# Second block's gate and up products with the weights stationary: 18 of 22 chunks in another form, no turns of their activations

## The reference, cut

```python
def swiglu(x, wg, wu, wd):
    return (jax.nn.silu(x @ wg) * (x @ wu)) @ wd
...
x = x + 0.5 * rms_norm(swiglu(rms_norm(x, g_ffn1_pre[l]), ffn1_wg[l], ffn1_wu[l], ffn1_wd[l]),
                       g_ffn1_post[l])
```

## Time and profile before

| | us |
|---|---|
| median of 3 runs | 2007.19 (2004.69 to 2007.57) |
| the profiled execution, its own time | 2004.62 |
| its span, first to last instruction | 2002.8 |
| PE busy | 1989.1 (99%) |
| DVE busy | 1209.0 (60%) |
| ACT busy | 991.7 (50%) |
| POOL busy | 300.8 (15%) |

### The profile page before, as it was taken

One profiled execution on the slowest core, in us unless ns is written; L12 is line 12 of the kernel. 1 busy time (PEld: TensorE's weight loads), 2 busy tenths in 40 slices (PEclk: granted clock), 3 DMA queues, 4 the chain that ended last, 5 costly groups with the idle time before them and its releaser, 6 DMA issues.

```text
span 2002.8 us, 26838 instructions
## 1 busy us (share of the span) xinstructions
PE 1989.1 (99%) x11298; PEld 1722.4 (86%) x11298; DVE 1209.0 (60%) x1163; ACT 991.7 (50%) x1076; POOL 300.8 (15%) x204
## 2 busy tenths in 40 slices
PE   9999999999999999999999999999999999999998
PEld 8899999999988888888888888888888888888887
DVE  6854446756677565546566875546555555686453
ACT  6754334345444454445366564445444535666443
POOL 4134401514244010002100110001000210011000
PEclk9999999999999999999999999999999999999999
DMA  7345546534555555555543545555555554364553
GB/s 224 106 130 183 171 172 209 170 127 148 174 185 188 191 187 188 189 192 167 188 128 125 199 158 185 185 198 168 189 180 198 168 168 147 120 208 152 183 179 136
DMA packets 195585, 343.64 MB, mean 172 GB/s; under 512 B 14122, under 2 KB 97356, under 8 KB 195356
## 3 DMA queue, kind: packets, MB, share of 16 engines
q1 hardware_dynamic: 194844, 340.12, 51.6%
q0 software_dynamic: 368, 0.79, 0.2%
q10 hardware_dynamic: 272, 1.26, 0.2%
HBM read 341.10 MB, written 1.05 MB: 171 GB/s over the span
## 4 chain that ended last, share of the span: by engine, by line
PE 88%; DVE 5%; ACT 3%; DMA 2%; issue 1%; POOL 1%; SPq 0%; DVEq 0%; POOLq 0%
PE banks L591 18%; PE banks L594 17%; PE banks L592 17%; PE banks L409 5%; PE banks L469 5%; PE banks L403 3%; PE banks L402 3%; PE banks L401 3%; PE banks L410 3%; PE banks L1833 2%; PE banks L1834 2%; PE banks L1835 2%; DVE w_lo L395 1%; ACT w_hi L379 1%; PE banks L630 1%; DVE xn_both L852 1%
## 5 line engine op out<-in xcount | busy, mean ns | idle before, releaser
L395 DVE TENSOR_TENSOR w_lo<-raw,w_hi 128x2048 fp32r<-128x2048 f32 x307 | 730.0, 2381 | 512.3 <-ACT w_hi L379 512.0
L379 ACT ACTIVATE w_hi<-raw 128x2048 fp32r<-128x2048 f32 x311 | 594.1, 1914 | 642.5 <-DMA raw<-ffn_wd 149.8
L591 PE MATMUL banks<-w_hi,xn_both 128*128 128x512 f32 x1192 | 472.0, 396 | 1.3 <-DVE xn_both L852 0.7
L592 PE MATMUL banks<-w_lo,xn_both 128*128 128x512 f32 x1192 | 464.1, 389 | 0.0
L594 PE MATMUL banks<-w_hi,xn_both 128*128 128x512 f32 x1192 | 459.6, 390 | 0.0
L591 PEld LDWEIGHTS banks<-w_hi,xn_both 128*128 128x128 f32 x1192 | 223.9, 188 | 50.4 <-DVE w_lo L395 3.1
L594 PEld LDWEIGHTS banks<-w_hi,xn_both 128*128 128x128 f32 x1192 | 223.8, 188 | 47.6
L592 PEld LDWEIGHTS banks<-w_lo,xn_both 128*128 128x128 f32 x1192 | 224.1, 188 | 44.0
L591 PE MATMUL banks<-w_hi,act_both 128*128 128x512 f32 x352 | 138.1, 392 | 0.0
L592 PE MATMUL banks<-w_lo,act_both 128*128 128x512 f32 x352 | 137.0, 389 | 0.0
L409 PE MATMUL banks<-xn_both,w_hi 128*128 128x512 f32 x352 | 123.5, 394 | 0.5 <-DVE ffn_u L1002 0.5
(11 more groups left out here) (384 smaller groups left out, 3348.7 us busy)
## 6 DMA issues: line engine op xcount, KB each, us to landing
raw<-w_in SPq DMA_DIRECT2D x58, 1024.0 KB, 5.1
raw<-ffn_wd SPq DMA_DIRECT2D x44, 1024.0 KB, 4.8
raw<-ffn_w_gu SPq DMA_DIRECT2D x42, 1024.0 KB, 5.0
raw<-ffn_wu SPq DMA_DIRECT2D x40, 1024.0 KB, 5.0
raw<-ffn_wg SPq DMA_DIRECT2D x35, 1024.0 KB, 5.0
raw<-ret_w_in SPq DMA_DIRECT2D x24, 1024.0 KB, 5.0
raw<-ffn_w_down SPq DMA_DIRECT2D x22, 1024.0 KB, 4.8
raw<-ret_w_out SPq DMA_DIRECT2D x8, 1024.0 KB, 5.3
```

The source lines that it names most:

```text
L379: nc.scalar.activation(hi_of(n0), raw_of(n0), ACT.Copy).then_inc(hi_done(n0), 1)
L395: nc.vector.tensor_tensor(lo_of(n0), raw_of(n0), hi_of(n0).bitcast(F32), ALU.subtract).then_inc(lo_done(n0), 1)
L591: pe.matmul(ps[:, (b + n) * 512:(b + n + 1) * 512], xh, h, start=start, stop=False)
L592: pe.matmul(ps[:, (b + n) * 512:(b + n + 1) * 512], xh, o, start=False, stop=False)
```

## The change

In each of the four feed-forwards chunks 4 to 21 (`NTILE` = 18) take the first block's form: a chunk is 1024 rows by 256 columns, even ones gate, odd ones up, and `tile_pair` issues 16 `joined` pairs into one pair of banks. Chunks 0 to 3 (the first 512 hidden columns) stay as they were, with the only `turn` that is left, after chunk 8. DVE, ACT and POOL get the first block's tile steps (`tile_gate`, `tile_up`, `tile_silu`, `tile_hi`, `pool_xffn`). They are placed in step c, behind the split of chunk c + 2, on tile c - 4, which is chunk c. The norm's factor is now needed along the free axis too, so there is a third matmul after chunk 3 with 256 columns, a square root and a reciprocal of 256 columns.

```diff
+            def tile_pair(n):
+                n0, b = base + 4 + n, ring(f, 2 + n)
+                wait_split(n0)
+                if n == 1:
+                    pe.wait_ge(S["gsil"], 2 * fi + 2)
+                elif n == 2:
+                    pe.wait_ge(S["gact"], 2 * fi + 2)
+                elif n:
+                    pe.wait_ge(S["sums"], x_sums(fi, n - 3))
+                for m in range(2):
+                    for kt in range(KT):
+                        last = joined(pe, b + m, slot_of(n0), kt * 256 + m * P, xn_both, slice(kt * T2, (kt + 1) * T2),
+                                      kt == 0, kt == KT - 1)
+                last.then_inc(S["pe_chunk"], 1)
...
-            for u in range(1, 11):
-                for q in range(2):
...
-                    if u >= 4 and u % 2 == 0 and q == 0:
-                        turn(u // 2 - 2)
...
+            pe.matmul(ps[:, 7 * 512 + T2:8 * 512], ones, sacc[:, 0:T2], start=False, stop=True, skip_group_check=True).then_inc(S["stat"], 1)
+            for n in range(NTILE):
+                tile_pair(n)
+                if n == 4:
+                    turn()
...
+                if k < 2:
+                    pe.wait_ge(S["fl"], 2 * fi + 2)
+                else:
+                    pe.wait_ge(S["al"], pair_count(fi, k - 2))
...
-                if k < 2:
-                    turn(4 + k)
...
+            def tile_silu(p):
+                act.wait_ge(S["g1"], pair_count(fi, p))
+                act.activation(xg[:, p % 2, :], xg[:, p % 2, :], ACT.Silu).then_inc(S["silu"], 1)
+
+            def tile_hi(p):
+                act.wait_ge(S["act"], pair_count(fi, p))
+                o = (4 + 2 * p) * T2
+                act.activation(act_hi[:, o:o + 2 * T2], xg[:, p % 2, :], ACT.Copy).then_inc(S["ah"], 1)
...
-                elif c in (6, 10, 14, 18, 22):
-                    silu((c - 2) // 4)
-                if c in (9, 13, 17, 21, 23, 24):
-                    hidden_hi((9, 13, 17, 21, 23, 24).index(c))
+                    silu()
+                if 4 <= c < 4 + NTILE:
+                    (tile_hi if c % 2 else tile_silu)((c - 4) // 2)
+                if c == 9:
+                    hidden_hi()
...
+            def leave(n, out):
+                dve.wait_ge(S["pe_chunk"], base + 4 + n + 1)
+                dve.tensor_reduce(out, bank(ring(f, 2 + n), 2).rearrange("p b (h t) -> p b t h", t=T2), AX.X, ALU.add).then_inc(S["sums"], 1)
+                dve.wait_ge(S["sums"], x_sums(fi, n))
+
+            def tile_gate(p):
+                if p >= 2:
+                    dve.wait_ge(S["al"], pair_count(fi, p - 2))
+                g = tiles(xg[:, p % 2, :], T2)
+                leave(2 * p, g)
+                dve.tensor_tensor(g, g, rep(rstd[:, 0:T2], 2, T2), ALU.mult).then_inc(S["g1"], 1)
+
+            def tile_up(p):
+                leave(2 * p + 1, tiles(xu[:, :], T2))
+                dve.wait_ge(S["silur"], pair_count(fi, p))
+                dve.tensor_tensor(xg[:, p % 2, :], xg[:, p % 2, :], xu[:, :], ALU.mult).then_inc(S["act"], 1)
...
+                    dve.reciprocal(rstd[:, 0:T2], std[:, 0:T2]).then_inc(S["sums"], 1)
                     dve.wait_ge(S["rstd"], s + 1)
...
+                    gated()
+                    dve.wait_ge(S["sums"], x_sums(fi, -1))
+                if 4 <= c < 4 + NTILE:
+                    (tile_up if c % 2 else tile_gate)((c - 4) // 2)
+                if c == 9:
+                    hidden_lo()
+
+        def pool_xffn(f):
+            for p in range(TPAIR):
+                g, v, o = xg[:, p % 2, :], pair_count(f - 2, p), (4 + 2 * p) * T2
+                pool.wait_ge(S["silu"], v)
+                pool.tensor_tensor(tiles(g, T2), tiles(g, T2), rep(rstd[:, 0:T2], 2, T2), ALU.mult).then_inc(S["silur"], 1)
+                pool.wait_ge(S["ah"], v)
+                pool.tensor_tensor(act_lo[:, o:o + 2 * T2], g, act_hi[:, o:o + 2 * T2].bitcast(F32), ALU.subtract).then_inc(S["al"], 1)
...
+            for n in range(NTILE):
+                at = 512 + 256 * (n // 2)
+                load(sp, base + 4 + n, 0, (uv if n % 2 else gv)[:, :, at:at + 256], (KT, 256))
```

More of the change, by code:

```diff
@@ L48 @@
 HEAD_SUMS = 4
+X_SUMS = HEAD_SUMS + 2 * NPAIR + KT
 AHEAD = 2
@@ new lines, in pe_xffn @@
+            for q in range(2):
+                for tb in range(2):
+                    if f > 2 and (q, tb) == (0, 0):
+                        continue
+                    last = quarter(base + 2 + q, 1, q, tb, False)
+                    if tb:
+                        last.then_inc(S["pe_chunk"], 1)
+                    elif q:
+                        last.then_inc(S["gmm"], 1)
+            if f == 2:
+                pe.wait_ge(S["hacc"], 8 * 4)
+            else:
+                pe.wait_ge(S["sa2"], 3 * (j + 1))
@@ L665, in pe_xffn @@
+            for tb in range(2):
+                pe.matmul(ps[:, 7 * 512 + 2 * tb:7 * 512 + 2 * tb + 2], sacc[:, tb * P:tb * P + P], ones[:, 0:2],
+                          start=(tb == 0), stop=True, skip_group_check=True)
+            pe.matmul(ps[:, 7 * 512 + T2:8 * 512], ones, sacc[:, 0:T2], start=False, stop=True, skip_group_check=True).then_inc(S["stat"], 1)
[3 more added lines that the diff above has]
+                    turn()
             a0, _, a1, _ = down_banks(f)
@@ L772, in gated, with hidden_lo @@
+                    dve.wait_ge(S["gsil"], 2 * fi + tb + 1)
+                    b = (ring(f, 1) + tb) * 512
+                    x = gs[:, tb, :]
+                    dve.scalar_tensor_tensor(out=x, in0=ps[:, b:b + 512], scalar=rcol[:, tb:tb + 1], in1=x, op0=ALU.mult,
                                              op1=ALU.mult).then_inc(S["gact"], 1)
-            def hidden_lo(g):
-                n = 4 if g < NGRP - 1 else 2
+            def hidden_lo():
                 for tb in range(2):
-                    dve.wait_ge(S["fh"], 12 * fi + 2 * g + tb + 1)
+                    dve.wait_ge(S["fh"], 2 * fi + tb + 1)
@@ L937, in sp_xffn @@
             base = BASE[f"gu{f}"]
-            for c in range(20):
+            for c in range(4):
                 if base + c in EXTRA:
                     continue
[L941 to L949, removed]
+                q, v = c % 2, uv if c >= 2 else gv
+                load(sp, base + c, 0, v[:, 4 * q:4 * q + 4, 0:512], (4, 512))
+            for n in range(NTILE):
+                at = 512 + 256 * (n // 2)
+                load(sp, base + 4 + n, 0, (uv if n % 2 else gv)[:, :, at:at + 256], (KT, 256))
             sp_wide(BASE[f"dn{f}"], w_dn.rearrange("(k p) c -> p k c", p=P), NDN, 0, 0)
```

79 lines of the change are left out of this document (35 added, 44 removed).

## The result

The changed kernel takes **2063.28 us** (median of 4 runs, 2060.0 to 2063.62), the kernel before 2007.38 beside it (median of 4, 2004.69 to 2007.98). The ratio is 1.0277, with a 95% interval of 1.0264 to 1.029: slower by 2.8%, where 2069 was forecast and 2055 to 2088 was the range. The profiled execution of the changed kernel took 2063.3 us, its span is 2061.5 us and its clock 0.996.

A forecast was written before the change was run, and what follows sets the result against it. TensorE's matmul count by spacing was taken to bound the kernel. A closed VectorE-ScalarE ring would add 15.5 us in each of four feed-forwards, +62 us: 2066.6 against the profiled execution, plus 2.6 for the median, forecast 2069 us, range 2055 to 2088.

The forecast's parts named there:

- What bounds the kernel before: Whole kernel: TensorE's matmul count by their spacing; chunks of 5.44 us in the old form, 5.55 in the new.
- PE's own count: TensorE per feed-forward: slower gate/up chunks, fewer transposes, one new norm product; -1.75 us each, -7 us in all.
- the product with the ones matrix: New 256-column norm matmul after chunk 3 in each feed-forward: 0.35 us taken as added.
- The ring: Gate/up chunks: VectorE drain, ScalarE tile step and high part, VectorE split, next drain wait in a circle; chance 0.86.
- The period: Time from drain to drain in the ring: 6.69 us gate, 6.83 up, mean 6.76, against TensorE's chunk of 5.55.
- Where it starts: gu3: VectorE free for the first drain at 1197.9 us, after the split, reciprocals and gated products.
- PE's waits: TensorE idles for w_lo about 1.2 us per chunk, from chunk 11 or 12 to 24 of each feed-forward.
- The clock: Rival: pauses drop TensorE to 1.2 GHz for a third of the ringed chunks; +87 us more, 2156 us; chance 0.02.
- The total: Four feed-forwards, gu2 to gu5, at +15.5 us each: +62 us, giving a forecast of 2069 us.
- the prediction's own bound of 7.1 us: Longest drain-to-drain time, with no overlap of neighbours and the full 1.36 and 0.83 us; 24 us more in all.

The follow-up runs named there:

- e2: Changed kernel with VectorE's tile step ahead of the split of chunk c + 2 from step 5, and hidden_lo behind that split; 1998.35 us, ratio 0.9965 to before.
- e1: Changed kernel with VectorE's tile step ahead of the split of chunk c + 2 from step 5, hidden_lo left in place; 2007.88 us, ratio 1.0008 to before.
- e3: Changed kernel with only ScalarE reordered: high part of chunk c + 3 ahead of the tile step of chunk c; 1998.39 us, ratio 0.9963 to before.
- e4: Changed kernel with one more ScalarE copy of 128 x 512 in every tile step, read by nobody; 2098.75 us.
- e5: e2 with the extra ScalarE copies of e4; 1999.13 us, ratio 0.9968 to the kernel before.
- e6: Changed kernel with both VectorE's order of e2 and ScalarE's order of e3; 2000.3 us, ratio 0.9968 to the kernel before.

## Why the prediction was right, point by point

- **What bounds the kernel before** held: chunk times by the starts (5.44, 5.55) came out again: 5.55 in the changed kernel (1221.11 - 1215.56, chunk 5) and in e2.
- **One reading was too strong**: that PE never waits for these steps in the first block. The earlier trace rows have one wait of 0.5 us, which the prediction names further on, and nothing hung on it.
- **PE's own count.** -1.75 us per feed-forward; e2, where nothing else is late, shows -1.77 in gu3. Inside, one term was a little too small: the product with the ones matrix was taken at 0.35 plus 0.1, and chunk 4 is 6.43 us from end to end (1215.56 - 1209.13) instead of 5.90 before, which is +0.53 with the 0.107 of the new form in it. So the product itself cost 0.42.
- **The ring** closed where it was said, through the steps that were said, and e1 to e3 show that the order closes it and e4 that its length is the chunk time.
- **The period** was the mis-sized term: 6.76 us forecast, 6.66 measured. The gate half was worked out at 6.69 and came at 6.64. The up half was at 6.89, of which 0.2 was the first block's longer way from reduction to product and silu; 0.14 of it was kept (6.83), so 0.07 in the mean of 6.76. In the unrolled code it is all gone (1.26 and 0.72 again). The other 0.03 is spread over the rows' distances, which came 0.01 to 0.03 shorter. 18 x 0.1 = 1.8 us per feed-forward too much.
- **Where it starts** came out by some luck. The first drain was set 6.7 us behind the end of chunk 3 (1197.9 - 1191.2), and came 7.1 behind (1216.22 against 1209.13). Under that lie two errors of opposite sign. The split of chunk 6, ahead of the first drain, was taken as in the kernel before, done 3.2 us behind the end of chunk 3, and was done 4.1 behind (1213.27), since ACT had waited for its load until 1209.11. The reciprocals and gated products behind it were given 3.5 us and took 2.95 (1216.22 - 1213.27); 0.15 of that is a slip, as the prediction's own terms from 1194.43 give 1197.75 and not 1197.9. From the first drain to the start of chunk 24: 120.9 us (forecast 122.8, with 1.1 for `hidden_hi`, measured 0.97 as the gap 1249.51 to 1257.14 less 6.66). From there to the end of chunk 28: 27.6 (forecast 27.5). Forecast 15.5, then +0.4, -1.9, +0.1 is 14.1.
- **PE's waits** began at chunk 12, as worked out.
- **The clock** did fall once, for about 3.4 us behind the 1.81 us wait in gu3, and it cost nothing, since the ring hid it: chunk 13 began without a wait, chunk 14 behind 0.22 instead of 0.84 us, and the drains stayed 6.66 apart. That is the self-limiting price which the rival named; its +87 us needed a fall in every third chunk, and took 11.1 us for a slow chunk, where 16 pairs at the measured 0.64 us make 10.2. The Trainium skill, page "TensorE: Matmul & The Clock Gate", section "A second HAM failure mode: psum-queue depth-cycling", tells of a bf16 kernel in which short pauses between groups of matmuls swing the clock. Here the regular pauses of 0.74 to 0.91 us never did: the granted clock is 1.00 over 1262 to 1337 us and over the same stretch of the other three feed-forwards.
- **The total**: 4 x 15.5 = 62 against 55.1 in these stretches, and 3.1 us of first-block time that no step foresaw, so 58.7 between the profiled executions. To 2066.6 another 2.6 was added, since the median before lay above its profiled run; the changed kernel's profiled run lay at its own median. That correction was of no use here; the last section has where such differences come from. The range's upper end of 2088 is 5 us below what the prediction's own bound of 7.1 us gives (2069 + 24), and the result didn't come near either.

gu4 and gu5 lose 0.6 us less than gu3, and the start of the ring accounts for it: their first drain comes 6.51 us behind the end of chunk 3 (6.94 in gu2, 7.09 in gu3), because ACT's high part of chunk 6, for which DVE's split waits, began 0.7 and 0.9 us ahead of that end (in gu5 the drain then still waited 0.18 us for PE). ACT in gu3 (chunk 3 ends at 1209.13) and in gu4 (at 1411.03):

```profile
1209.11 1.91 ACT L383 ACTIVATE w_hi<-raw 128x2048 fp32r<-128x2048 f32 x1 [5.11 <-DMA raw<-ffn_wg]
...
1410.32 1.92 ACT L383 ACTIVATE w_hi<-raw 128x2048 fp32r<-128x2048 f32 x1 [0.92 <-DMA raw<-ffn_wg]
```

ACT could start on this chunk 5.8 us after the load's issue in gu3 (1203.29), and 5.2 and 5.0 us after it in gu4 and gu5. Why the load took longer there is open.

## What to carry to other kernels

When two in-order engines feed each other, write down for one item the chain "A waits for B's result of c, B's next result stands behind A's result of c + k", and add the durations along it: that sum, divided by the number of items that one trip gets ahead, is the least time per item, and the busy share of either engine doesn't show it. Here 6.66 us for one item stood against 5.55 of PE, with DVE 63% and ACT 48% busy. It takes both orders to close such a ring, so moving one step on either engine (release the producer's buffer first, then prepare further ahead) opens it, as one trip then serves two items; here that was worth 65 us of 2063 with no instruction changed. An added dummy step tells whether a ring is closed: in the closed one it cost all of its 0.52 us each time, in the open one nothing.

## What the runs showed of the hardware

**Two spacings of the same pairs.** The same joined pairs, in unchanged code, stand 0.3467 us apart in one execution and 0.3533 in another. SP's issue times in gu1 (22 gate/up chunks) and its down product (11), of before:

```profile
513.12 119.67 SPq L367 DMA_DIRECT2D raw<-ffn_w_gu  x22
637.83 55.84 SPq L367 DMA_DIRECT2D raw<-ffn_w_down  x11
```

and of the changed kernel:

```profile
513.87 121.69 SPq L371 DMA_DIRECT2D raw<-ffn_w_gu  x22
640.71 56.91 SPq L371 DMA_DIRECT2D raw<-ffn_w_down  x11
```

10 chunks of 16 pairs in the second row: 55.84 against 56.91 is 0.107 per chunk, 0.0067 per pair; both rows together are 3.1 us. The profiled executions of e2, e3 and e5 have the short value (1998.21, 1998.39 and 1998.61 us), that of e6 the long one (2001.14 us), with the same work. So executions of one kernel differ by some 3 us, as 2004.69 and 2007.57 of before may; those were not traced one by one. Within one execution it can change at a wait: in e1's gu3 the chunks end 5.55 us apart ahead of the 1.17 us wait and 5.65 behind it:

```profile
1230.42 0.37 SPq L371 DMA_DIRECT2D raw<-ffn_wu  x1
1235.97 0.37 SPq L371 DMA_DIRECT2D raw<-ffn_wg  x1
1243.05 0.37 SPq L371 DMA_DIRECT2D raw<-ffn_wu  x1
1248.71 0.37 SPq L371 DMA_DIRECT2D raw<-ffn_wg  x1
```

It need not: in e1's gu5, behind the same wait (1.16 us, at 1879.45), they stay 5.54 apart:

```profile
1885.30 0.37 SPq L371 DMA_DIRECT2D raw<-ffn_wu  x1
1890.84 0.37 SPq L371 DMA_DIRECT2D raw<-ffn_wg  x1
```

The price of the wait differs by that. From chunk 3 to 28 gu3 is 142.3 us there against 139.7 in e2, so one wait of 1.17 us cost 2.6; in gu5 it cost 1.4. All four together are 9.3 us, about what the medians differ (9.5). A wait isn't needed either: in e2's gu2 the pairs go from 0.347 to 0.353 us at 745.5, where no wait is shown, and chunks 6 to 8 last 5.65 us each; from the turn on they are back at 5.55. What decides is open: in gu1 both the changed kernel and e2 had a wait of 0.70 us, and they came out with different values.

**The clock behind a single wait.** Windows of the changed kernel in gu3 (length, busy time by engine, then granted clock, DMA share, GB/s), around the 1.81 us wait that ends at 1257.27:

```profile
1250.00:1257.00 7.00, 5.46 (x32) 4.53 (x30) 4.78 (x5) 3.41 (x4) 1.30 (x1) 1.00 0.52 161
...
1258.00:1261.50 3.50, 3.50 (x13) 3.02 (x12) 1.04 (x2) 2.39 (x2) 1.29 (x1) 0.52 0.57 202
1262.00:1270.00 8.00, 8.00 (x47) 6.97 (x46) 5.46 (x4) 2.44 (x2) 1.30 (x1) 1.00 0.41 131
```

The granted clock is 0.52 of full, the 1.2 GHz level, and pairs stand 0.64 us apart. It fell behind this wait, and in e4 behind three of the four waits of 2.2 to 2.3 us (window 1269.9 to 1272.0: 0.50). Behind none of the others that were looked at did pairs slow down: 1.46, 1.47 and 1.72 us in the changed kernel, 1.17 in e1, the regular 1.25 to 1.36 of e4. In the closed ring such a fall is hidden. No run here shows one in an open kernel, where PE has no slack to hide it in.

**GpSimd under VectorE's split.** The prediction allowed POOL 2.3 to 2.6 us per product, from the first block. In the ring it took half of that, since DVE is idle just then. POOL in the changed kernel:

```profile
1259.82 1.29 POOL L844 TENSOR_TENSOR xg<-xg,rstd 128x512 f32<-128x512 f32 x1 [6.32 <-ACT xg L751]
```

and in e2, with the split of DVE beside it:

```profile
1238.29 2.29 DVE L399 TENSOR_TENSOR w_lo<-raw,w_hi 128x2048 fp32r<-128x2048 f32 x1
...
1239.11 2.61 POOL L848 TENSOR_TENSOR act_both<-xg,act_both 128x512 fp32r<-128x512 f32 x1 [2.86 <-ACT act_both L756]
```

The product ends at 1241.72, 1.14 us behind the split's end (1240.58). In the earlier trace rows the first pair of them ends 1.15 us apart too (602.11 + 2.31 = 604.42 against 600.98 + 2.29 = 603.27), though it overlapped the split for another length. So POOL seems to stand still until the split is done, which these ends suggest and no run tested. DVE pays nothing: its split takes 2.29 us either way. The Trainium skill, page "SBUF — State Buffer", section "Who interferes with whom", says that a DVE instruction with two SBUF inputs contends with a GpSimd one that reads SBUF. These rows agree: the product takes 1.0 to 1.3 us more with the split beside it (2.31 and 2.61 against 1.29).
